# Value products over a side-by-side high|low stationary operand in a split-fp32 diffusion step

## The reference, cut to what matters

```python
def one_block(qblk):
    sc = jnp.einsum('bqgrd,btgd->bgrqt', qblk, k).astype(jnp.float32) * scale
    p = jax.nn.softmax(sc, axis=-1).astype(v.dtype)
    return jnp.einsum('bgrqt,btgd->bqgrd', p, v)
...
o = jnp.concatenate([o_mla.reshape(b, s, -1), o_na.reshape(b, s, -1), o_gqa.reshape(b, s, -1)], axis=-1)
return o @ w_out
...
xs = xs + g_a * mix_out(o_mla, o_na, o_gqa, w_out[l])
xs = xs + g_f * swiglu(modulate(xs, norm_ffn_g[l], sh_f, sc_f), w_gate[l], w_up[l], w_down[l])
```

## Time and profile before

| | before |
|---|---|
| median of 3 runs | 1892.22 us (1890.54 to 1901.45) |
| profiled execution, whole | 1892.63 us |
| its span | 1890.8 us |
| attention stage, layer 0 and 1 | about 205 to 422 and 1113 to 1330 us |
| PE, DVE, ACT, POOL busy | 1715.8, 1171.3, 699.0, 216.2 us |

### The profile page before, as it was taken

How to read it: one execution, slowest core, us unless ns; L and a number is a source line. 1 busy time by engine, 2 the same in 40 slices (tenths; PEclk the granted TensorE clock), 3 DMA queues, 4 the chain that set the end, 5 groups by cost and what they waited for, 6 DMA issues and landing times.

```text
span 1890.8 us, 29170 instructions
## 1 busy us (share of the span) xinstructions
PE 1715.8 (91%) x11708; PEld 1662.6 (88%) x11708; DVE 1171.3 (62%) x2233; ACT 699.0 (37%) x1381; POOL 216.2 (11%) x314
## 2 busy tenths in 40 slices
PE   4589778889899999999989977899989999999997
PEld 4589667779899999999989966777889999999997
DVE  5999667873677677676652257788364444544444
ACT  2423655772522221122243356578252222112222
POOL 0000625220000000000010053523000000000001
PEclk9999789999899999999989988999989999999998
DMA  9364100014234434333122010000412222222201
GB/s 329 132 229 145 33 1 2 1 26 153 90 132 167 146 121 157 122 122 122 42 74 80 29 41 0 1 3 23 129 50 67 83 73 67 84 93 67 67 22 55
DMA packets 107912, 159.82 MB, mean 85 GB/s; under 512 B 4976, under 2 KB 85680, under 8 KB 107568
## 3 DMA queue, kind: packets, MB, share of 16 engines
q1 hardware_dynamic: 105024, 152.52, 24.1%
q0 software_dynamic: 640, 2.92, 0.6%
q10 hardware_dynamic: 2160, 3.23, 0.5%
HBM read 155.08 MB, written 3.57 MB: 84 GB/s over the span
## 4 chain that ended last, share of the span: by engine, by line
PE 75%; DVE 15%; ACT 5%; issue 3%; POOL 2%; ACTq 1%; DVEq 0%; POOLq 0%
PE ps L571 23%; PE ps L572 23%; PE ps L573 23%; DVE ps L1217 6%; PE ps L778 2%; DVE negmax L1419 1%; PE ps L757 1%; DVE K L1202 1%; DVE hT L1202 1%; PE ps L635 1%; PE ps L759 1%; PE ps L579 1%; DVE pT L1202 1%; DVE Q L1313 1%; POOL rstd L1574 1%
## 5 line engine op out<-in xcount | busy, mean ns | idle before, releaser
L571 PE MATMUL ps<-hT,gw 128*128 128x320 f32 x1408 | 437.0, 310 | 6.8 <-DVE hT L1202 6.8
L572 PE MATMUL ps<-hT,gw 128*128 128x320 f32 x1408 | 436.7, 310 | 0.0
L573 PE MATMUL ps<-hT,gw 128*128 128x320 f32 x1408 | 436.6, 310 | 0.0
L1281 DVE SCALAR_TENSOR_TENSOR x<-ps,mod,x 128x320 f32<-128x320 f32 (+2 forms) x576 | 211.9, 434 | 123.9 <-PE ps L573 120.9
L571 PEld LDWEIGHTS ps<-hT,gw 128*128 128x128 f32 x1408 | 265.9, 189 | 7.3 <-issue 7.3
L572 PEld LDWEIGHTS ps<-hT,gw 128*128 128x128 f32 x1408 | 265.8, 189 | 0.0
L573 PEld LDWEIGHTS ps<-hT,gw 128*128 128x128 f32 x1408 | 265.8, 189 | 0.0
L1507 DVE TENSOR_TENSOR mm<-sl,ps 128x320 f32<-128x320 f32 x88 | 42.7, 487 | 318.0 <-issue 185.3
L571 PE MATMUL ps<-act,dw 128*128 128x320 f32 x704 | 219.0, 311 | 2.7 <-DVE act L1202 2.7
L572 PE MATMUL ps<-act,dw 128*128 128x320 f32 x704 | 218.7, 311 | 0.0
L573 PE MATMUL ps<-act,dw 128*128 128x320 f32 x704 | 218.6, 311 | 0.0
(11 more groups left out here) (197 smaller groups left out, 3608.0 us busy)
## 6 DMA issues: line engine op xcount, KB each, us to landing
gw_raw<-in_w_gate SPq DMA_DIRECT2D x22, 1024.0 KB, 5.5
gw_raw<-in_w_up SPq DMA_DIRECT2D x22, 1024.0 KB, 8.0
dw_raw<-in_w_down SPq DMA_DIRECT2D x22, 1024.0 KB, 4.9
ada_w<-in_w_adaT SPq DMA_DIRECT2D x42, 512.0 KB, 6.0
ada_wf<-in_w_adaT SPq DMA_DIRECT2D x34, 512.0 KB, 6.8
wi_raw<-in_w_in SPq DMA_DIRECT2D x16, 912.0 KB, 5.5
ada_wq<-in_w_adaT SPq DMA_DIRECT2D x20, 512.0 KB, 4.1
wo_raw<-in_w_out SPq DMA_DIRECT2D x16, 512.0 KB, 4.3
```

What stands on the lines that cost most here:

```text
L571: pe.matmul(dst, lh, rh, start=start, stop=False, skip_group_check=True)
L572: pe.matmul(dst, lh, rl, start=False, stop=False, skip_group_check=True)
L573: return pe.matmul(dst, ll, rh, start=False, stop=stop, skip_group_check=True)
L1281: i = ve.scalar_tensor_tensor(out=x[:, o, c0:c1], in0=ps[:, banks + hf_, s0:s0 + c1 - c0], scalar=mod[:, l, part * KD + o, q:q + 1], in1=x ...
```

## The change

V becomes `V[:, pair, tile, slot, 128]`: for the first head 64 high columns and then 64 low ones, for the second head 64 low and then 64 high. That is the stationary operand as it stands; two passes, one over pT high and one over pT low, give both V high x p and V low x p in the two halves of the partitions (the product low x low is now among them). The zeros and their memset go. The two heads of a pair no longer share an accumulation: bank 6 is emptied after each head. ACT copies it raw to `o_raw[:, slot]`; two SBUF to SBUF DMAs on SP bring each head's other half across the partitions into `o_sum`; POOL adds the halves (two instructions on 64 partitions); ACT copies the sum to hT high; POOL subtracts for hT low. The last pair goes another way: ACT copies its crossing halves straight from PSUM, and DVE adds and subtracts, but for the first head's 512 columns, which go by a DMA and a POOL add. PE's waits for hT become waits for the raw copies.

```diff
@@ schedule
-        if k > 10 and k % 10 == 1:
-            order += [("OL", k // 10 - 1), ("OP", k // 10 - 1)]
         if prompt:
             order.append(("TP", k // 10 - 1))
         order += extra[2 * n]
         if 0 <= k < len(trans):
             order.append(trans[k])
+        if k >= 5 and k % 5 == 0:
+            order.append(("OL", k // 5 - 1))
         if prompt:
-            order.append(("OF", k // 10 - 1))
+            order += [("OF", k // 10 - 1), ("OP", k // 10 - 1)]
         order += extra[2 * n + 1]
-    order += [("OL", NP - 1), ("OP", NP - 1)]
+        if k >= 10 and k % 10 == 1:
+            order.append(("OA", k // 10 - 1))
+        if k >= 10 and k % 10 == 2:
+            order.append(("OH", k // 10 - 1))
+    order += [s for s in (("OA", NP - 1), ("OH", NP - 1)) if s not in order]
+    order.insert(order.index(("OL", NH - 1)), ("OB", NP - 1))
@@ SP
+                    if s[0] == "OP" and s[1] < NP - 1:
+                        pair = s[1]
+                        sp.wait_ge(o_out, l * 3 * NP + 3 * pair + 3)
...
+                        sp.dma_start(o_sum[0:64, :], o_raw[64:P, 0, :]).then_inc(o_moved, 16)
+                        sp.dma_start(o_sum[64:P, :], o_raw[0:64, 1, :]).then_inc(o_moved, 16)
@@ PE, pv
-                                if pair > 0:
-                                    pe.wait_ge(o_ready, l * 2 * NP + 2 * pair - 1)
+                            if mt == 0 and g > 0:
+                                pe.wait_ge(o_out, l * 3 * NP + 3 * ((g - 1) // 2) + (g - 1) % 2 + 1)
...
-                            lh, ll = (V[:, pair % 2, q, vt, 64 * slot:64 * slot + P] for q in range(2))
-                            m = split_mm(ps[:, 6, c0:c1], lh, ll, pT_at(n, 0, c0, c1), pT_at(n, 1, c0, c1),
-                                         slot == 0 and mt == 0, False)
+                            for q in range(2):
+                                m = pe.matmul(ps[:, 6, c0:c1], V[:, pair % 2, vt, slot, :], pT_at(n, q, c0, c1),
+                                              start=mt == 0 and q == 0, stop=mt == 4 and q == 1, skip_group_check=True)
@@ PE, pvp
-                            prev7[0] = (o_ready, 2 * NP, 2 * pair + 2)
+                            prev7[0] = (o_out, 3 * NP, 3 * pair + 3)
@@ ACT
+                            sc.activation(o_raw[:, g % 2, 0:LAT], ps[:, 6, :], ACT.Copy).then_inc(o_out, 1)
...
+                            sc.activation(o_raw[:, :, LAT:T], ps[:, 7, 0:2 * P].rearrange("p (a b) -> p a b", a=2),
+                                          ACT.Copy).then_inc(o_out, 1)
+                    elif s[0] == "OH":
+                        sc.wait_ge(o_added, l * 2 * NP + 2 * s[1] + 2)
+                        sc.activation(hT[:, PAIR_TILE[s[1]], 0, :], o_sum[:], ACT.Copy).then_inc(o_hi, 1)
@@ DVE
+                    elif s == ("OA", NP - 1):
...
+                        ve.tensor_tensor(o_sum[64:P, 0:LAT], ps[64:P, 6, :], o_sum[64:P, 0:LAT], ALU.add)
@@ POOL
-                po.memset(bass.AP(tensor=zeros.tensor, offset=zeros.offset, ap=[list(zeros.ap[0]), [192, 24], [1, 64]]),
-                          0.0).then_inc(vz_done, 1)
+                    elif s[0] == "OA" and s[1] < NP - 1:
+                        po.wait_ge(o_moved, 16 * (l * (2 * NP - 1) + 2 * s[1] + 2))
...
+                        for slot in range(2):
+                            r = slice(64 * slot, 64 * slot + 64)
+                            po.tensor_tensor(o_sum[r, :], o_raw[r, slot, :], o_sum[r, :], ALU.add).then_inc(o_added, 1)
+                            po.wait_ge(o_added, l * 2 * NP + 2 * s[1] + slot + 1)
+                    elif s[0] == "OH" and s[1] < NP - 1:
+                        o_lo(po, l, s[1])
```

More of the change, by code:

```diff
@@ L193, in build @@
         pT3 = sb("pT3", [P, 2, 512], F32R, s0)
+        o_sum = sb("o_sum", [P, T], F32, s0)
         s0.close()
@@ L276, in build @@
         s5.close()
-        V = sb("V", [P, 2, 2, 6, 192], F32R)
+        V = sb("V", [P, 2, NT + 1, 2, P], F32R)
+        o_raw = sb("o_raw", [P, 2, T])
         K = sb("K", [P, 2, 2, KEYS], F32R)
@@ L356, in build @@
         pv_done = sem("pv_done")
+        o_out = sem("o_out")
+        o_moved = sem("o_moved")
+        o_added = sem("o_added")
         o_hi = sem("o_hi")
@@ L395, in v_slots @@
         def v_slots(pair, q, t0, n):
-            v = V[:, pair % 2, q, t0:t0 + n, :]
-            return bass.AP(tensor=v.tensor, offset=v.offset, ap=[list(v.ap[0]), [192, n], [128, 2], [1, 64]])
+            v = V[:, pair % 2, t0:t0 + n, 0, 64 * q:P]
+            return bass.AP(tensor=v.tensor, offset=v.offset, ap=[list(v.ap[0]), [2 * P, n], [64 if q else 192, 2], [1, 64]])
         def v_sources(g, q):
@@ L408, in v_sources @@
                 cache = vc_na if kind == "na" else vc_g
-                d0 = 128 * slot
-                res.append((V[:, pair % 2, q, 0:NT, d0:d0 + 64], z[:, 0:NT, c0:c0 + 64], V[:, pair % 2, 0, 0:NT, d0:d0 + 64]))
-                res.append((V[:, pair % 2, q, 5, d0:d0 + 64], cache[:, cc:cc + 64], V[:, pair % 2, 0, 5, d0:d0 + 64]))
+                d0, hi0 = 64 * (q ^ slot), 64 * slot
+                res.append((V[:, pair % 2, 0:NT, slot, d0:d0 + 64], z[:, 0:NT, c0:c0 + 64], V[:, pair % 2, 0:NT, slot, hi0:hi0 + 64]))
+                res.append((V[:, pair % 2, 5, slot, d0:d0 + 64], cache[:, cc:cc + 64], V[:, pair % 2, 5, slot, hi0:hi0 + 64]))
             return res
@@ L453, in reciprocals, with o_lo @@
                 ve.reciprocal(rinv[:, w:w + 1], rsum[:, w:w + 1]).then_inc(rinv_ready, 1)
+        def o_lo(eng, l, pair):
+            eng.wait_ge(o_hi, l * NP + pair + 1)
+            o = PAIR_TILE[pair]
+            eng.tensor_tensor(hT[:, o, 1, :], o_sum[:], hT[:, o, 0, :].bitcast(F32), ALU.subtract).then_inc(o_ready, 1)
         def norm_unit(po, l, u):
@@ L524, in _ @@
                 for s in SCHED:
+                    if s[0] == "OP" and s[1] < NP - 1:
+                        pair = s[1]
+                        sp.wait_ge(o_out, l * 3 * NP + 3 * pair + 3)
+                        if pair or l:
+                            sp.wait_ge(o_ready, l * NP + pair)
+                        sp.dma_start(o_sum[0:64, :], o_raw[64:P, 0, :]).then_inc(o_moved, 16)
+                        sp.dma_start(o_sum[64:P, :], o_raw[0:64, 1, :]).then_inc(o_moved, 16)
+                    if s == ("OL", NH - 2):
+                        sp.wait_ge(o_out, l * 3 * NP + 3 * (NP - 1) + 1)
+                        sp.wait_ge(o_ready, l * NP + NP - 1)
+                        sp.dma_start(o_sum[0:64, 0:LAT], o_raw[64:P, 0, 0:LAT]).then_inc(o_moved, 16)
                     if s[0] == "GZ" and s[1] == NT - 1:
@@ L812, in pvp @@
                             for slot in range(2):
-                                lh, ll = (V[:, pair % 2, q, 4, 64 * slot:64 * slot + P] for q in range(2))
                                 c0, c1 = slot * P, (slot + 1) * P
-                                m = split_mm(ps[:, 7, 0:P], lh, ll, pT_at(n, 0, c0, c1), pT_at(n, 1, c0, c1),
-                                             slot == 0, slot == 1)
+                                for q in range(2):
+                                    m = pe.matmul(ps[:, 7, c0:c1], V[:, pair % 2, 4, slot, :], pT_at(n, q, c0, c1),
+                                                  start=q == 0, stop=q == 1, skip_group_check=True)
                             m.then_inc(pv_done, 1)
-                            prev7[0] = (o_ready, 2 * NP, 2 * pair + 2)
+                            prev7[0] = (o_out, 3 * NP, 3 * pair + 3)
                         pending.append(pvp)
+                    elif s[0] == "OL" and s[1] == NH - 1:
+                        flush(1)
                     elif s[0] == "OF":
@@ L823, in _ @@
                         misc_step(l, *s[1:])
-                pe.wait_ge(o_ready, l * 2 * NP + 2 * NP)
+                pe.wait_ge(o_ready, l * NP + NP)
                 for o in range(KD):
@@ L1430, in _ @@
                         lo(pT_at(n, 1, c0, c1), ps[:, 4 + n % 2, c0:c1], pT_at(n, 0, c0, c1)).then_inc(pT_ready, 1)
[L1431 to L1435, removed]
+                    elif s == ("OA", NP - 1):
+                        ve.wait_ge(o_out, l * 3 * NP + 3 * NP - 1)
+                        ve.tensor_tensor(o_sum[64:P, 0:LAT], ps[64:P, 6, :], o_sum[64:P, 0:LAT], ALU.add)
+                        ve.wait_ge(o_out, l * 3 * NP + 3 * NP)
+                        ve.tensor_tensor(o_sum[0:64, LAT:T], ps[0:64, 7, 0:P], o_sum[0:64, LAT:T], ALU.add)
+                        ve.tensor_tensor(o_sum[64:P, LAT:T], ps[64:P, 7, P:2 * P], o_sum[64:P, LAT:T], ALU.add).then_inc(o_added, 1)
+                    elif s == ("OH", NP - 1):
+                        o_lo(ve, l, NP - 1)
                     elif s[0] == "C":
@@ L1632, in _ @@
                             norm_unit(po, l, u)
+                            scaled += 1
+                    elif s[0] == "OA" and s[1] < NP - 1:
+                        po.wait_ge(o_moved, 16 * (l * (2 * NP - 1) + 2 * s[1] + 2))
```

(14 more changed lines are left out.)

27 lines of the change are left out of this document (16 added, 11 removed).

## The result

The changed kernel takes 1964.53 us (median of 4, 1962.93 to 1966.29) against 1892.31 us before: ratio 1.0367, 95% interval 1.0339 to 1.0395. It is slower by 72 us; the forecast was 1881. The profiled execution took 1962.9 us, its span 1960.9.

A forecast was written before the change was run, and what follows sets the result against it. No engine was far ahead; value passes were mostly on the path, with write-outs at pair ends. Per layer -12 - 5.5 + 3 + 7.5 + 1.4 = -5.6, -11 in two layers: 1881 us, forecast 1872 to 1889, 8-in-10 range 1862 to 1902.

The forecast's parts named there:

- The handover, +7.5: At pair ends, ScalarE's output copy waits for DMAs and GpSimd adds: 2.0 us in two gqa pairs, 0.7 in five before.
- the waits for hT, -5.5: TensorE's waits for VectorE's hT low at pair ends go: -5.5 us a layer, bounds 0 and 9.2.
- Third passes, -12 a layer: Attention value products lose their third pass: about 18 us of TensorE's time, -12 us a layer on the path.
- Two thirds: Share of dropped pass time that shortens the path, from the chain's 5.9 of 9.2 us in the last 60 us.
- second rival: In attention, VectorE holds the pace, so only 3 of the passes' 12 us are had: 1893 us, chance 0.20.
- Engines about level, +3: In attention, three engines about level wait for each other in every slot: +3 us a layer, between 0 and 9.
- The clock rival: A 7.0 us handover leaves TensorE idle at late pairs and its clock falls: +20 a layer, 1932 us, chance 0.10.
- Tail, +1.4: After the last pair, extra copies, adds and the output copy delay the projection: +1.4 us a layer.
- Memset, 0: Dropping the memset of V saves nothing, as GpSimd's next instruction waited 2.96 us more for a DMA.
- the signs I had listed: Expected in the attention profile: each add 1.5 us, and no TensorE waits for hT before the last pair.
- 0.5 inside mla or gqa: A granted clock of 0.5 in these attention heads would show the forecast wrong; 1.00 was expected in gqa.
- the attention was not 211 us long: Expected sign: the attention stage of a layer about 211 us long, from 217 us before.

The follow-up runs named there:

- the profile with 0.91 above: Kernel before with the third value pass left out in the mla and gqa heads only, kept in the four na heads; the run again measured 1876.45 us.
- 98 repeats a layer: Changed kernel with 14 repeats of the last value pass in each of TensorE's seven idle stretches a layer before the output copy; 1945.42 us, ratio 1.0266.

## Why the prediction was wrong, by its own steps

Two steps failed. The handover, +7.5 a layer, was mis-sized: the wait at OH is worth 29 us in the two layers alone and 40 with the other stall gone. And the waits for hT, -5.5, had 0 as the worst bound, where what took their place, ScalarE's wait at the first head's raw copy, is worth 30 to 40. Beside them the passes gave 3 us where 24 were forecast.

**Third passes, -12 a layer.** The count and the price of a pass were right: 128 value passes of 512 columns stand where 192 did.

```profile
L821 PE MATMUL ps<-pT,V 128*128 128x512 f32 x128 | 50.7, 481 | 0.0
```

The step from TensorE's time to the path failed. "Two thirds", read from the chain's share of L573, is too much. It was also worked out wrongly: of the 40 passes in those 60 us eight have 128 columns, so they are 7.8 us and not 9.2, and the chain's 5.9 are three quarters. Measured are the passes of heads 4 to 15 (60 of 512 and 12 of 128 columns, some 14.5 us of TensorE). From the second TP to the last, at a clock of 1.00 in both kernels (the profile with 0.91 above), they shorten a layer from 141.0 to 135.3 us: 5.7 us, two fifths. The medians give 7 to 8 a layer. A likely reason is that a chain names one last engine per step, though VectorE was 0.2 us behind it (15.8 against 16.0 of 18 us). With the na heads' passes gone too, a lower clock in those heads took the gain back. Together -1 to -2 a layer. My second rival's "three of the twelve" was nearest, by another mechanism.

**Waits for hT, -5.5.** They went, but the price paid in their stead was outside my bounds, which ended at 0. I wrote that the raw copies stand ahead of an exponential, a slot earlier, and did not ask at which slot the product that they copy is executed. The answer stood in `flush(1)`: one slot behind its place in the list. This is worth 30 us in two layers, 40 with the handover's stall gone.

**Engines about level, +3.** Not seen by itself. With all stalls moved away the new exchange against the kernel before with two passes is +4 us in two layers with the additions in a row, and -7 with them apart (by the ratios). So ScalarE's 11.5 us of new work a layer cost little at most; what cost was GpSimd's order of work, 11 us in two layers, which I had called hidden in its idle time. That step looked at GpSimd's sum of busy time, not at what is queued behind 3.1 us of additions.

**Handover, +7.5.** The durations were right: the adds take 3.14 us a pair, a DMA 2.6 us instead of 2.4 (issues of the changed kernel: KB, us to landing).

```profile
o_sum<-o_raw SPq DMA_DIRECT2D x14, 160.0 KB, 2.6
```

Wrong was when ScalarE comes. I took two mean slots, 3.6 us. From the end of the raw copy at 407.41 to the end of what it did before OH (the copy to pT) it took 2.7 us: the exponentials behind a pair's end followed each other in 1.4 us. Before, too, two of them there stood at 390.34 and 391.69. And a pair's handover runs in the first slots of the next pair, so three of the seven run at gqa's pace, and not the two that I counted. And the chain of 5.5 us took 6.3, as the second DMA is issued half a us behind the first. So 3.6 us of standing in each of the last three of the seven pairs, instead of 1.9 in two, and 1.4 to 2.9 in the four before them, where I had 0.7 a pair: 18.7 us in all. Moving OH is worth 29 us alone and 40 with the other stall gone; of this, 19 us or more are the clock.

**The clock rival** (1932 us, chance 0.10) had the right sign, place and mechanism for the handover's half of the loss: a hole of 4.3 us and a granted clock of 0.50, the level of 1.2 GHz, behind it in gqa. Its condition, "if the handover takes 7.0 us", was too strict: 6.3 did it. With the mid-pair stall removed, the kernel is at 1935. That this is so near 1932 is in part luck, as the rival counts 24 us for the passes. The Trainium skill's rule on bursts with waits between them ("TensorE: Matmul & The Clock Gate", section "HAM oscillation — how this bites in real kernels"), on which I kept the chance low, agrees with these traces: 0.83 over the attention against 0.93.

**Tail, +1.4.** TensorE stands 6.12 us before the projection, 4.18 before: +1.9. From the last TP to the projection it is 8.1 us against 6.7, the +1.4 forecast. **Memset, 0:** nothing speaks against it. The adds' duration and the missing waits for hT came as the signs I had listed; "0.5 inside mla or gqa", listed as a sign of error, came too, and the attention was not 211 us long but some 33 us longer than before.

## What to carry to other kernels

An instruction moved ahead of others on an in-order engine must be checked against the slot in which its input is really executed (pending work, a DMA and the adds behind it), and against what stands behind it in the queue: here four places in a list were worth 79 us, the change itself about 10. Take the arrival time from the timeline at that very place, not from a mean slot. Before trading work for hops between engines, price the removed work by a kernel that only leaves it out; that run would have shown 3 us where 24 were forecast.

## What the runs showed of the hardware that was not expected

- Work put into a hole can give time back through the clock: 98 repeats a layer (7 x 14, 23 us of TensorE), 19 us less in all.
- The same instructions can meet two clocks: the kernel before and the two with fewer passes from head 4 or from head 8 on are the same up to the end of the second na pair, and this pair takes 36.1 to 36.3 us in two of their profiles and 40.6 to 41.7 in two others. Executions of one kernel fall in two groups 9 us apart (1876 and 1885), with the mean clock (0.965 and 0.957).
- Work left out went with more time: 48 passes fewer in the na heads of two layers, 11 to 15 us more, at a lower clock. Whether the passes did it stays open.
- A POOL addition on 64 partitions takes as long as on 128 (1.57 us each in a pair of them, 1.56 for 128x640).
